# Another order of outputs, sums of squares and reciprocals in the retention of a hybrid retention, Fourier and PEER layer

## What is computed

```
scores = (q k^T) * decay_mask
out    = scores v + (q * q_decay) state        # forward and backward
ret    = out * rsqrt(mean(out^2 over the head's 64 channels) + 1e-6)
mix    = ret * ret_gain * silu(gate)
y      = concat(mix, fourier) @ w_out
```

## Time and profile before

| | us |
|---|---|
| median of 3 runs | 1428.14 |
| lowest and highest run | 1421.80, 1428.81 |
| profiled execution, its own time | 1425.9 |
| span of the profiled execution | 1424.1 |
| granted TensorE clock, mean | 0.999 |

### The profile page before, as it was taken

One profiled execution on the slowest core, in us unless ns is written; L12 is line 12 of the kernel. 1 busy time (PEld: TensorE's weight loads), 2 busy tenths in 40 slices (PEclk: granted clock), 3 DMA queues, 4 the chain that ended last, 5 costly groups with the idle time before them and its releaser, 6 DMA issues.

```text
span 1424.1 us, 22569 instructions
## 1 busy us (share of the span) xinstructions
PE 1396.8 (98%) x8225; PEld 1227.4 (86%) x8225; DVE 1204.0 (85%) x2671; ACT 586.9 (41%) x888; POOL 774.1 (54%) x541
## 2 busy tenths in 40 slices
PE   8999999999999999999999999999999999999998
PEld 4888877788899999999999999788888888888886
DVE  5787869767899979999996797888888888898987
ACT  4433144633434434555554443443433333333333
POOL 0230100014569996655657855487876776777760
PEclk9999999999999999999999999999999999999999
DMA  9872333225369998899999979999999999999993
GB/s 376 308 276 90 119 134 102 61 74 165 98 209 330 322 318 283 297 392 388 382 404 387 396 295 359 399 413 416 418 416 369 390 410 402 407 403 406 414 401 152
DMA packets 165061, 440.82 MB, mean 310 GB/s; under 512 B 14832, under 2 KB 63728, under 8 KB 164976
## 3 DMA queue, kind: packets, MB, share of 16 engines
q1 hardware_dynamic: 74048, 195.52, 37.2%
q0 software_dynamic: 51264, 186.67, 34.1%
q10 hardware_dynamic: 39664, 57.58, 10.8%
HBM read 398.40 MB, written 41.29 MB: 309 GB/s over the span
## 4 chain that ended last, share of the span: by engine, by line
PE 74%; DVE 10%; DMA 8%; ACT 3%; POOL 2%; issue 2%; SPq 1%; another core or an unknown queue 0%; ACTq 0%; DVEq 0%; POOLq 0%
PE ps L1979 23%; PE ps L1980 23%; PE ps L1981 23%; DMA blk_raw<-u_t 5%; DVE rows L1730 2%; PE ps L2386 1%; DMA rows<-u_nat,ids 1%; DVE ws_lo L1891 1%; DMA ada_w<-w_ada 1%; ACT ws_hi L1116 1%; PE ps L2325 1%; DMA rows<-u_nat,few_row_ids 1%; POOL rows L788 1%; PE ps L1996 1%; DVE one_plain L1855 0%
## 5 line engine op out<-in xcount | busy, mean ns | idle before, releaser
L1979 PE MATMUL ps<-vs_hi,coef_hi 128*128 128x512 f32 x768 | 299.0, 389 | 2.0 <-DVE coef_lo L1936 2.0
L1980 PE MATMUL ps<-vs_lo,coef_hi 128*128 128x512 f32 x768 | 298.8, 389 | 0.0
L1981 PE MATMUL ps<-vs_hi,coef_lo 128*128 128x512 f32 x768 | 298.8, 389 | 0.0
L1979 PE MATMUL ps<-hT_hi,ws_hi 128*128 128x320 f32 (+1 forms) x832 | 275.0, 331 | 3.6 <-DVE ws_lo L1891 2.3
L1981 PE MATMUL ps<-hT_hi,ws_lo 128*128 128x320 f32 (+1 forms) x832 | 269.9, 324 | 0.0
L1980 PE MATMUL ps<-hT_lo,ws_hi 128*128 128x320 f32 (+1 forms) x832 | 269.9, 324 | 0.0
L1730 DVE CUSTOM_DVE_ANT_0 rows<-rows,ps 128x1024 f32<-128x1024 f32 x192 | 226.4, 1215 | 26.5 <-DMA rows<-u_nat,ids 15.3
L823 POOL TENSOR_TENSOR vs_lo<-blk_raw,vs_hi 128x1024 fp32r<-128x1024 f32 x60 | 144.8, 2413 | 84.1 <-DVE coef_lo L1936 83.8
L788 POOL DMA_INDIRECT rows<-u_nat,ids x128 | 144.4, 1128 | 56.4 <-DVE sp_act L1730 26.7
L1170 ACT ACTIVATE vs_hi<-blk_raw 128x1024 fp32r<-128x1024 f32 x128 | 135.0, 1055 | 92.5 <-PE ps L1981 83.1
L1979 PEld LDWEIGHTS ps<-vs_hi,coef_hi 128*128 128x128 f32 x768 | 144.1, 188 | 32.8 <-DVE coef_lo L1936 2.8
(11 more groups left out here) (359 smaller groups left out, 2695.3 us busy)
## 6 DMA issues: line engine op xcount, KB each, us to landing
blk_raw<-u_t SPq DMA_DIRECT2D x128, 512.0 KB
blk_raw<-v_nat SPq DMA_DIRECT2D x128, 512.0 KB
g_dram<-g_buf ACTq DMA_DIRECT2D x124, 160.0 KB
grp_g<-g_dram ACTq DMA_DIRECT2D x31, 640.0 KB
w_dram<-w_stage SPq DMA_DIRECT2D x32, 512.0 KB
grp_w<-w_dram ACTq DMA_DIRECT2D x31, 512.0 KB
part_w<-w_ada POOLq DMA_DIRECT2D x24, 512.0 KB, 6.0
raw<-w_in SPq DMA_DIRECT2D x20, 512.0 KB, 6.2
```

Source lines behind the costliest of these rows:

```text
L1979: pe.matmul(o, lh, rh, start=start, stop=False, skip_group_check=True)
L1980: pe.matmul(o, lh, rl, start=False, stop=False, skip_group_check=True)
L1981: return pe.matmul(o, ll, rh, start=False, stop=stop, skip_group_check=True)
```

## The change

The same instructions in another order on three engines.

On VectorE, masks 0 and 1 move ahead of `rest_four(3)`; `decayed(2)` and `decayed(3)` move between masks; all eight masks stand ahead of the first mean square; mean squares 0 and 1 stand together ahead of `inverse(0)`; `rest_unit(20)` to `(23)` each move one place ahead among inverses and norms. On TensorE, `outputs(0)` and `outputs(1)` go between score pairs, `gains(1)` and `sum_squares(0)` come behind the last score pair, and sums of squares 1 and 2 come one output later. On ScalarE, the squares of pairs 0 and 1 and of 2 and 3 stand together, and units 20 to 23 are rounded at other places among the roots.

```diff
@@ ScalarE
             take_gain(0)
             square(0)
+            square(1)
+            take_gain(1)
             root_ret(0)
-            square(1)
+            root_ret(1)
             round_unit(20)
-            root_ret(1)
             square(2)
-            take_gain(1)
+            square(3)
             root_ret(2)
-            square(3)
             round_unit(21)
+            root_ret(3)
             round_unit(22)
-            root_ret(3)
+            round_unit(23)
             round_ret(0)
             round_ret(1)
-            round_unit(23)
             round_ret(2)
             round_ret(3)
@@ VectorE
             rest_four(2)
-            rest_four(3)
...
-            for h in range(HEADS - 1):
-                masked(h)
+            masked(0)
+            masked(1)
+            rest_four(3)
+            masked(2)
+            masked(3)
+            decayed(2)
+            masked(4)
+            masked(5)
+            decayed(3)
+            masked(6)
+            masked(7)
             mean_square(0)
-            decayed(2)
+            mean_square(1)
             inverse(0)
-            masked(HEADS - 1)
-            mean_square(1)
-            decayed(3)
+            rest_unit(20)
             inverse(1)
             mean_square(2)
-            rest_unit(20)
+            rest_unit(21)
             inverse(2)
             mean_square(3)
-            rest_unit(21)
+            rest_unit(22)
             norm((0, 1))
-            rest_unit(22)
             inverse(3)
+            rest_unit(23)
             norm((2, 3))
             norm_rest((0, 1))
-            rest_unit(23)
             norm_rest((2, 3))
@@ TensorE
             gains(0)
             score_pair(1)
+            outputs(0)
             score_pair(2)
-            outputs(0)
+            outputs(1)
             score_pair(3)
+            gains(1)
             pe.wait_ge(four_l, GROUPS)
             sum_squares(0)
-            outputs(1)
-            sum_squares(1)
             pe.wait_ge(gg_step, 1)
             outputs(2)
-            gains(1)
-            sum_squares(2)
+            sum_squares(1)
             pe.wait_ge(gg_step, 2)
             outputs(3)
+            sum_squares(2)
```

## The result

Changed kernel: median 1431.81 us over 22 runs (1426.48 to 1439.36); before, 1428.24 over 22 runs (1421.32 to 1434.74). The ratio is 1.0027, 95% interval 1.0014 to 1.0040: 3.9 us slower, with 2.0 to 5.7 in the interval (the two medians are 3.6 us apart). The forecast was +4.6 us and 1432.

A forecast was written before the change was run, and what follows sets the result against it. TensorE's progress was the bound, its stage end hanging on when VectorE starts reciprocals and releases small results. Projection start -1.9, waits +2.4, +3.1, +0.9: +4.5 us (+4.6 by list), 1432.7 on the median, put at 1432; range 1426 to 1437.

The forecast's parts named there:

- Masks 0 and 1 early: Both masks move into VectorE's 1.98 us idle time, so score pair 1 starts at 201.1 without waiting; gain 1.4 us.
- Outputs between score pairs: On TensorE, waits ahead of score pairs 2 and 3 go; outputs 3 end at 219.3; alone, 3.9 us gained on TensorE.
- Reciprocals behind all masks: VectorE idles 3.4 us ahead of mean square 1; inverse 0 starts 4.2 us later, at 217.0; net lag 1.9 us.
- what is late next: Inside unit 20, mean squares 2 and 3 come late; VectorE's remainders 21 and 22 each wait 1.8 us for ScalarE's rounding.
- Waits inside the projection: TensorE waits 2.4 us for mean square 2, 3.1 for mean square 3, and 0.9 for a norm in unit 22.
- TensorE's clock, costed at nothing: Earlier trace kept full clock through a 2.36 us wait, so the 3.1 us wait was priced at nothing, a fall not excluded.
- rival C: TensorE's clock falls in the new waits, behind the 3.1 us one: +4.4 us at halfway, 1436 to 1437; chance 0.10.
- A granted clock that drops between 221 and 245: Sign of being wrong: TensorE's clock leaving full speed inside the projection, where the forecast had no fall.
- Nothing comes back later: Behind unit 24 no independent clock takes up the 4.6 us of delay; costed at nothing.
- Rival B: The stall is real but absorbed further on by a transfer or GpSimd's gain of gg_last: 1428 us; chance 0.10.
- Rival A: TensorE's waits of 1.37, 0.91 and 0.70 us go and the projection runs through: -3.0 us, 1425; chance 0.07.
- Rival D: Reorder only hides waits; stalls inside unit 20 are shorter than laid out by 2 us or more: 1429 to 1430; chance 0.08.

The follow-up runs named there:

- e4_masks_early: Kernel before with only masks 0 and 1 moved ahead of the last Fourier block's remainder; unit 24 at 244.92, ratio to before 0.9989.
- e8_pe_only: Kernel before with TensorE's order as changed, VectorE's and ScalarE's as before; unit 24 at 254.51, ratio to before 1.0039.
- e2_inverse_between: Changed kernel with inverse 0 ahead of mean square 1 on VectorE, one swap; unit 24 at 250.14, ratio to before 1.0022.
- e11_after_again: Changed kernel run and profiled once more with no edit; unit 24 at 250.62, ratio to before 1.0035.
- e3_both: Changed kernel with inverse 0 ahead of mean square 1 and ScalarE's roundings ahead of the roots; unit 24 at 245.88, ratio to before 0.9984.
- e7_order: New order: the changed kernel's early masks and outputs between score pairs, reciprocals started early, ScalarE as before; unit 24 at 244.83, ratio to before 0.9970.
- e5: Changed kernel with unit 21's first three groups ahead of unit 20's last group on TensorE; unit 24 at 252.00, ratio to before 1.0045.
- e9: Changed kernel with TensorE's order as before, VectorE's and ScalarE's as changed; unit 24 at 263.15, ratio to before 1.0110.
- e10: Changed kernel with two and three products adding zeros in TensorE's two waits inside unit 20; unit 24 at 250.55, ratio to before 1.0026.

## Why the prediction held, step by step

- *Masks 0 and 1 early, gain 1.4 us*: right. Score pair 1 starts at 201.12 (laid out 201.1); alone, the part gives 1.3 us (e4_masks_early).
- *Outputs between score pairs*: right on TensorE. Outputs 3 end at 219.06 (219.3). But it is a gain only with VectorE's order to match: alone it costs 8.3 us at unit 24 (e8_pe_only).
- *Reciprocals behind all masks, "here the gain is lost"*: the numbers were right (idle 3.17 us against 3.4, first reciprocal 216.90 against 217.0), the weight was not. Taking that wait away gives back 0.5 us (e2_inverse_between). I had listed ScalarE's roundings behind the roots under what is late next, as a follower of the lag; they are at least half of the cause. Removing their waits gives 2.7 us and removing both 4.7, which is all of the lag of 4.4 and more.
- *Waits inside the projection, 2.4, 3.1 and 0.9 us*: 2.24, 2.72 and 0.52 in the brackets of e11_after_again, at a full clock. A bracket leaves out the 0.17 us by which the matmul ahead overlaps its neighbour and the 0.1 us by which the first one behind a wait is longer (0.50 against 0.39); with these it is 2.5, 3.0 and 0.8. Less the 1.9 us by which the projection starts sooner, that is the 4.4 us from 246.20 to 250.62. Laid out: 250.8. So the mechanism and the positions are confirmed to 0.2 us. The time alone is weak evidence: its interval, 2.0 to 5.7 us, would have held 3 as well as 4.6.
- *TensorE's clock, costed at nothing, rival C at 0.10*: this is the term that the prediction had wrong. In the profiled execution the fall did come, in the wait that rival C named, at 1.9 us instead of its halfway 4.4: the slow stretch ended at 237.97, with 14 matmuls affected, and the wait for the norm took up some of it. A granted clock that drops between 221 and 245 was one of the prediction's own signs of being wrong, and that sign appeared; it did not in the second profile of the same kernel. By the mean clocks (0.9978 for the change, 0.9985 for the kernel before on that chip) half speed lasts 2.0 us longer per execution on average, an estimate: twice 0.0007 of 1429 us; it costs half of that, 1.0 us. In the 22 executions of the result the mean clock is 0.9968. That the time still landed at 3.9 us, with this term missing from the sum of 4.6, is partly luck.
- *Nothing comes back later*: right. 1177.7 us behind unit 24 against 1177.9. But this stretch is not constant: 1176.2 in e11_after_again (span 1426.8), 1181.1 in e3_both (1427.0), where half speed from 614 to 621, behind a wait of 3.05 us, is in it. A single span can't judge an order here; the position of unit 24 can. Rival B, that all is absorbed, falls by the times too: the interval starts at 2.0 us.
- *Rival A* was false as forecast for this order, but its price of 3.0 us was near what a suitable order yields (2.2 in e7_order). Its condition, inverse 0 by about 213.9, was nearly met in e2_inverse_between (214.21), and mean square 3 came only 0.3 us sooner (230.83 against 231.17): the 15.1 us that the prediction put between the two contain the waits for ScalarE, which don't move along. *Rival D* fell: the waits came to within 0.1 us each, in the same terms.

## What to carry to other kernels

When engines run fixed orders, lay all the queues side by side and look for a long operation (here a 3.3 us reciprocal) queued behind a short one that waits for another engine; then do it again with that wait removed, because the next queue (here ScalarE's rounding behind a root) is often waiting directly behind and keeps the time. Covering the waiting engine with other work shows whether its wait is the cost or only where the cost is seen. An order is good or bad as a set: TensorE's part alone put unit 24 back by 8.3 us, VectorE's and ScalarE's by 17.0 (falls of the clock included in both), and all three together by 4.4 to 6.3.

## What the runs showed of the hardware

With two waits of TensorE of 2.24 and 2.73 us in the stage, the clock fell to half speed in one profile (the mean clock of 0.57 over 8 us is 6.9 us of it) and not in another of the same kernel. The wait of the earlier trace rows itself, 2.36 us at full clock before, has 2.38 us in the changed kernel's profile, and there the clock is 0.69 behind it, the nine products behind it 2.18 us instead of 1.20. TensorE's timeline and the windows of the changed kernel:

```profile
552.03 2.18 PE L2404 MATMUL ps<-ident,picks 128*128 128x128 f32 x9 [2.38 <-DVE picks L1810]
```

```profile
545.00:550.00 5.00, 4.64 (x32) 4.38 (x30) 4.93 (x8) 1.85 (x3) 2.67 (x2) 1.00 1.01 385
550.00:555.00 5.00, 2.97 (x13) 2.98 (x14) 4.90 (x9) 3.70 (x5) 3.42 (x2) 0.69 0.49 166
```

No order here touches that place. In the thirteen profiles this wait is 2.23 to 3.32 us long, and the clock falls in or behind it in nine; before, e5, e9 and e10 are the four without a fall. So one profile at full clock is no evidence that a wait of 2 us or more is free of a fall, and the row on which I costed the clock at nothing was the rarer case. And a plain fp32 product 512 columns wide takes 0.86 us, two records, where an fp32r one of the projection takes 0.227 us: filling TensorE's waits with the former needs few of them.
